# Query rotation on GpSimd, v's token shift inside the first key choice, the third gate pair as rounded products

## The reference

```python
p = x @ w_in                                   # attention, gate and RWKV columns
c_q = rms_norm(cq_raw, g_cq)
q  = partial_rope((c_q @ w_uq).reshape(B, S, 8, 128), *rope_a)   # first 32 of 128 rotated
qi = partial_rope((c_q @ w_iq).reshape(B, S, 8, 64), *rope_i)
score = sum over heads of relu(qi . ki) * wi ; _, idx = lax.top_k(score, 64)
y_a = softmax(q . k[idx]) @ v[idx] @ w_oa
p_rw = p + (prev_token(p) - p) * mu            # token shift of r, k, v, w, a, g
y_b = rwkv7_time_mix(...)                      # the recurrence, in rounds below
g_a, g_b = sigmoid(p_gate + b_gate)            # 2 x 1024 gate columns
x = layer_norm(alpha * x + (g_a * y_a + g_b * y_b) @ w_out)
x = layer_norm(alpha * x + conv_glu_ffn(x))
```

## Time and profile before

| | |
|---|---|
| median of 3 runs | 1107.33 us |
| the profiled execution, its own time | 1107.22 us |
| span of the profile, first to last instruction | 1105.4 us |
| TensorE busy | 1077.7 us, 97% |
| VectorE busy | 802.7 us, 73% |
| ScalarE busy | 569.6 us, 52% |
| GpSimd busy | 72.2 us, 7% |
| mean granted TensorE clock | 0.995 of full speed |

### The profile page before, as it was taken

How to read it: one execution, slowest core, us unless ns; L and a number is a source line. 1 busy time by engine, 2 the same in 40 slices (tenths; PEclk the granted TensorE clock), 3 DMA queues, 4 the chain that set the end, 5 groups by cost and what they waited for, 6 DMA issues and landing times. The chain is left out here.

```text
span 1105.4 us, 31915 instructions
## 1 busy us (share of the span) xinstructions
PE 1077.7 (97%) x13568; PEld 977.2 (88%) x13568; DVE 802.7 (73%) x1471; ACT 569.6 (52%) x1008; POOL 72.2 (7%) x61
## 2 busy tenths in 40 slices
PE   8999999999999999999999999999999999999996
PEld 8878888888997999998898888888888979999885
DVE  3678787868676877774557887878876778777645
ACT  3653555555544555553246445555565445555531
POOL 0000010101001000000100000202011010000001
PEclk9999999999999999999999999999999999999998
DMA  8533232322564666566474323222326637566661
GB/s 302 166 102 118 72 101 80 95 90 89 191 229 135 211 190 189 186 200 197 134 236 142 121 88 98 89 86 81 98 64 229 210 128 226 189 185 189 210 188 56
DMA packets 45526, 165.58 MB, mean 150 GB/s; under 512 B 5168, under 2 KB 5424, under 8 KB 45136
## 3 DMA queue, kind: packets, MB, share of 16 engines
q1 hardware_dynamic: 42736, 154.03, 43.4%
q0 software_dynamic: 1504, 7.47, 2.2%
q10 hardware_dynamic: 1152, 2.10, 0.6%
HBM read 160.44 MB, written 3.15 MB: 148 GB/s over the span
## 5 line engine op out<-in xcount | busy, mean ns | idle before, releaser
L771 PE MATMUL ps<-x_tok_r,mid_hi 128*128 128x256 f32 x576 | 177.1, 307 | 0.5 <-DVE ring_r L1758 0.5
L773 PE MATMUL ps<-x_tok_r,ring_r 128*128 128x256 f32 x576 | 162.2, 282 | 0.0
L772 PE MATMUL ps<-yb_hi,mid_hi 128*128 128x256 f32 x576 | 162.1, 281 | 0.0
L1758 DVE TENSOR_TENSOR ring_r<-ring,mid_hi 128x1024 fp32r<-128x1024 f32 x80 | 97.2, 1216 | 31.1 <-ACT mid_hi L1342 31.0
L771 PEld LDWEIGHTS ps<-x_tok_r,mid_hi 128*128 128x128 f32 x576 | 108.5, 188 | 9.5 <-issue 1.4
L772 PEld LDWEIGHTS ps<-yb_hi,mid_hi 128*128 128x128 f32 x576 | 108.9, 189 | 0.7 <-issue 0.7
L773 PEld LDWEIGHTS ps<-x_tok_r,ring_r 128*128 128x128 f32 x576 | 108.9, 189 | 0.0
L1342 ACT CAST mid_hi<-ring 128x1024 fp32r<-128x1024 f32 x80 | 83.8, 1048 | 34.3 <-PE ps L773 26.6
L2021 DVE TENSOR_TENSOR rs_ks_r<-ring,tha_kkn_r 128x1024 fp32r<-128x1024 f32 x44 | 53.9, 1224 | 19.9 <-ACT tha_kkn_r L1394 19.7
L2021 DVE TENSOR_TENSOR vs_dC_r<-ring,b_k_r 128x1024 fp32r<-128x1024 f32 x44 | 53.7, 1220 | 17.6 <-ACT b_k_r L1394 17.6
L2021 DVE TENSOR_TENSOR X_Y_r<-ring,arc_r 128x1024 fp32r<-128x1024 f32 x42 | 51.3, 1222 | 19.8 <-ACT arc_r L1394 19.8
(11 more groups left out here) (487 smaller groups left out, 3326.0 us busy)
## 6 DMA issues: line engine op xcount, KB each, us to landing
ring<-stream_dram SPq DMA_DIRECT2D x281, 512.0 KB, 3.7
lora_w<-lora_dram POOLq DMA_DIRECT2D x2, 1536.0 KB, 7.2
W_bt<-rpar_dram POOLq DMA_DIRECT2D x4, 512.0 KB, 5.1
kt_V<-rpar_dram POOLq DMA_DIRECT2D x4, 512.0 KB, 7.1
x_tok<-x_dram SPq DMA_DIRECT2D x2, 512.0 KB, 4.7
v_saved_dram<-vs_dC ACTq DMA_DIRECT2D x4, 256.0 KB, 4.5
x_tok<-x_dram SPq DMA_DIRECT2D x1, 1024.0 KB, 6.2
vf<-v_saved_dram ACTq DMA_DIRECT2D x4, 256.0 KB, 3.8
```

The lines of the kernel that those rows point to most:

```text
L771: pe.matmul(dst, lh, rh, start=start, stop=False)
L772: pe.matmul(dst, lh, rl, start=False, stop=False)
L773: return pe.matmul(dst, ll, rh, start=False, stop=stop)
L1758: dve.tensor_tensor(rounded["ring"][:, k, :], ring[:, k, :], f32(mid_hi[m % NM][:, :]), ALU.subtract).then_inc(*dve_mid.inc(l, m))
```

## The change

Constants: `PLAIN_GATES = 2` is new; `MIDS` takes gate slots from 4 on (6 before), so the third gate pair is multiplied in the rounded way, and `FIRST_MIDS` is 10 (8 before). The two additional splits stand on ACT behind the exponentials and ahead of the first gate's tanh; on DVE the first is in the middle of the second key choice, the second right behind it and ahead of `prep_keys`. The two rotations of the queries go from DVE to POOL, which reads and writes the same buffers; TensorE's wait ahead of the query transposes is on POOL. v's token shift, which stood ahead of the first key choice, is now done ahead of its sixth step.

```diff
-FIRST_MIDS = 2 + 3 * GB
+PLAIN_GATES = 2
+FIRST_MIDS = 2 + 3 * GB + 2 * (GATES_FIRST - PLAIN_GATES)
...
-MIDS = [s for s in SLOTS if s[1] == "gate" and s[2] >= 2 * GATES_FIRST or s[1] == "rkv" and s[2] % KB >= GB
+MIDS = [s for s in SLOTS if s[1] == "gate" and s[2] >= 2 * PLAIN_GATES or s[1] == "rkv" and s[2] % KB >= GB
...
+            def queries(l, j):
+                pool.wait_ge(*act_att(l, f"q{j}"))
+                pool.wait_ge(*(pool_att(l, "rq0") if j else dve_att(l, "rqi")))
...
+                pool.tensor_tensor(t[0], x1, cos, ALU.mult)
+                pool.tensor_tensor(t[1], x2, sin, ALU.mult)
+                pool.tensor_tensor(t[2], x2, cos, ALU.mult)
+                pool.tensor_tensor(t[3], x1, sin, ALU.mult).then_inc(*pool_att.inc(l, f"rq{j}a"))
+                pool.wait_ge(*pool_att(l, f"rq{j}a"))
+                pool.tensor_tensor(x1, t[0], t[1], ALU.subtract)
+                pool.tensor_tensor(x2, t[2], t[3], ALU.add).then_inc(*pool_att.inc(l, f"rq{j}"))
...
+                queries(l, 0)
+                queries(l, 1)
                 head_norm(GROUPS * l)
...
-                pe.wait_ge(*dve_att(l, "rq1"))
+                pe.wait_ge(*pool_att(l, "rq1"))
...
                 prep_exp(r0)
+                mids_up_to(l, FIRST_MIDS)
                 gate(l, 0)
...
-                    queries(0)
                     scores_of(4)
                     scores_of(5)
-                    queries(1)
...
-                rkv(l, 0, 2)
...
-                topk(0)
+                topk(0, lambda: rkv(l, 0, 2))
...
-                topk(1, lambda: prep_rn(r0))
+                topk(1, lambda: (prep_rn(r0), mids_up_to(l, FIRST_MIDS - 1)))
+                mids_up_to(l, FIRST_MIDS)
                 prep_keys(r0)
```

More of the change, by code:

```diff
@@ L532, in trunk @@
                                          + scores(0) + scores(1)
-                                         + (scores(2) + scores(3) + rope("rq0") + scores(4) + scores(5) + rope("rq1") if l else
-                                            rope("rq0") + scores(2) + scores(3) + rope("rq1") + scores(4) + scores(5))
+                                         + scores(2) + scores(3) + scores(4) + scores(5)
                                          + sum([[f"causal{t}"] + sum([[f"max{t}{i}", f"rep{t}{i}"] for i in range(8)], [])
@@ L538, in trunk @@
                                          for l in L2])
-        pool_att = by_layer("pool_att", ["eps", "rs"])
+        pool_att = by_layer("pool_att", ["eps", "rs"] + rope("rq0") + rope("rq1"))
         pe_prep = Steps(sem("pe_prep"), [(["ss", "zw", "za"] if r % GROUPS else ["zw", "za", "ss"]) + (["zv"] if r >= GROUPS else []) + ["rnT", "rnx"]
@@ L664, in norm_rsqrt @@
                                        ).then_inc(*pool_x.inc(l, f"{w}{t}"))
+            def queries(l, j):
+                pool.wait_ge(*act_att(l, f"q{j}"))
+                pool.wait_ge(*(pool_att(l, "rq0") if j else dve_att(l, "rqi")))
+                n = TT * 4 * 16
+                t = [yt[:, :, :].rearrange("p u s -> p (u s)")[:, 0:n], sq[:, :, :].rearrange("p u s -> p (u s)")[:, 0:n],
+                     *[X_Y[:, i, :, :].rearrange("p u s -> p (u s)")[:, 0:n] for i in range(2)]]
+                t = [a.rearrange("p (t h f) -> p t h f", t=TT, h=4) for a in t]
+                sin, cos = [sines[:, i, :, 0:16].unsqueeze(2).broadcast_to([P, TT, 4, 16]) for i in range(2)]
+                qv = q_tok[j].rearrange("p t (h f) -> p t h f", h=4)
+                x1, x2 = qv[:, :, :, 0:16], qv[:, :, :, 16:32]
+                pool.tensor_tensor(t[0], x1, cos, ALU.mult)
[5 more added lines that the diff above has]
+                pool.tensor_tensor(x2, t[2], t[3], ALU.add).then_inc(*pool_att.inc(l, f"rq{j}"))
             def head_norm(r):
@@ L1598, in _ @@
                     scores_of(3)
-                    mids_up_to(l, FIRST_MIDS)
+                    mids_up_to(l, 2 + 3 * GB)
                     queries(0)
@@ L2242, in index_queries @@
                     rotate(l, "rqi", qv[:, :, :, 0:8], qv[:, :, :, 8:16], 16, 8, H_IDX).then_inc(*dve_att.inc(l, "rqi"))
[L2244 to L2248, removed]
                 def scores_of(i):
```

## The result

The changed kernel takes 1114.57 us, the median of 7 runs (1112.53 to 1116.35), against 1106.68 us for the kernel before in the same comparison (7 runs, 1104.95 to 1110.11). The ratio is 1.0066, interval 1.0047 to 1.0085: slower by 5.2 to 9.4 us. A second comparison of the same two kernels gave 1.0056 [1.0036, 1.0077]. The forecast was slower, 1111.5 us; the measured median lies 0.4 us above the upper end of its range. The profiled execution took 1113.22 us, its span is 1111.4.

A forecast was written before the change was run, and what follows sets the result against it. TensorE's list was taken to set the time, with DVE's chain level beside it; 1.0 + 0.1 + 1.23 + 1.8 = +4.1 us on the median 1107.33 gave 1111.5 us, range 1109.3 to 1114.2.

The forecast's parts named there:

- The DVE chain: DVE's list up to the keys: 2.30 us of subtractions less 1.07 gained; +1.0 us in layer 0, +1.23 in layer 1.
- The products: Third gate pair on TensorE: rounded products save 0.69 us per slot, 2.8 in all, but the saving turns into waiting.
- POOL: Query rotations on POOL take 3.3 us per half; TensorE waits 0.1 us in layer 0 and 1.8 in layer 1.
- The sum: All waits over both layers: 1.0 + 0.1 + 1.23 + 1.8 = +4.1 us.
- rival 1: POOL's second-half rotation and DVE's sums in layer 0 exclude each other, up to 2.1 us: 1113.6 us; chance 0.15.
- Rival 2: POOL rotates as quickly as DVE, 1.42 us per half, so neither layer waits for it: +2.2 us, 1109.5; chance 0.18.
- Rival 3: DVE not held by TensorE's steps; second key choice begins 2.4 us earlier: 1106.9 or 1108.9 us; chance 0.04.

The follow-up runs named there:

- a3: Kernel before with only the third gate pair as rounded products, both subtractions on DVE, rotations and v's shift as before: ratio 1.0072.
- b2: Changed kernel with the third gate pair's two subtractions on POOL instead of DVE: ratio 1.0023 against the kernel before.
- b3: Changed kernel with the two subtractions on POOL and the second query half's rotation back on DVE: ratio 1.0002 against the kernel before.
- c1: Changed kernel; in layer 0 DVE's sums of s4 and s5 wait until POOL has rotated the second query half: one execution, 1116.05 us.
- a1: Kernel before with one edit, v's token shift moved into the first key choice: ratio 0.9992.
- c3: a1 run once more, unaltered: ratio 0.9992 against the kernel before.
- a2: Kernel before with both query rotations on POOL, nothing else changed: ratio 1.0000.
- c2: Kernel before, third gate pair plain, with two long-fulfilled waits ahead of each of its 16 products in both layers: ratio 0.9996.
- b1: Changed kernel with the second query half rotated on DVE again, the first half still on POOL: ratio 1.0065 against the kernel before.
- b4: Changed kernel with 60 long-fulfilled semaphore waits at the very start of TensorE's list: ratio 1.0074 against the kernel before.
- a4: Kernel before with 96 long-fulfilled semaphore waits in TensorE's list while it waits for the first input: ratio 1.0021.
- d1: The changed kernel unaltered, run once more: ratio 1.0056 against the kernel before.

## Why the prediction was right, and where its size was off

**The DVE chain.** The forecast was 1.0 us for layer 0 and 1.23 for layer 1. In layer 0 1.25 in all were measured, of which 0.11 are POOL, so 1.14; in layer 1 2.49 less 1.23 for POOL, so 1.26. The second key choice began near where it was put (78.83, less the later start of 0.37 is 78.46; forecast 78.30), held by the sums of squares. The first one ended 0.5 us later than forecast (75.28 - 0.37 = 74.91 against 74.4), since DVE's sums and the first row behind them were slower beside POOL; that used up the wait for the tanh in layer 0 and cost nothing more. a3 shows the same from the other side: without the rotations' gain the two subtractions cost 2.15 and 2.28 us, that is their 2.30 less the small slack of layer 0. b2 and b3, where DVE is rid of them, turn the sign in layer 0 (-1.03 and -1.19).

**The products.** 24 of them took from 86.84 to 89.7 us, 2.9 us as forecast, with a wait of 0.39 us between the slots and 1.56 ahead of the grams; the forecast was 0.5 and 1.7.

**POOL.** The sum's terms were 0.1 us for layer 0 and 1.8 for layer 1; measured 0.11 and 1.23. The term of layer 1 was too large: undisturbed, a sum of 128 elements takes no longer than a product, and steps are 0.42 us each, 2.67 us for a half, where the line from the 128x512 rows gave 3.3. POOL's first and last row of that half in layer 1 of the changed kernel:

```profile
614.08 0.46 POOL L677 TENSOR_TENSOR yt<-gates,sines 128x128 f32<-128x128 f32 x1 [1.92 <-ACT gates L1592]
...
616.29 0.46 POOL L683 TENSOR_TENSOR gates<-X_Y 128x128 f32<-128x128 f32 x1
```

That layer 0 was right was luck: there the half took 3.28 us because DVE's sums lay beside it. So rival 1 is real in kind, at 0.6 us and not 2.1, and hardly visible in the total since TensorE arrives at that moment anyway. The Trainium skill, SBUF — State Buffer, section Who interferes with whom, calls the contention on the ports that VectorE and GpSimd share an exclusive lock. c1 shows the contention. But if each of the four DVE operations of 0.5 us had locked POOL out for its whole length, POOL would have lost nearly 2 us (an estimate from these rows), and it lost 0.6.

**The sum.** +4.1 was forecast for the stages and +3.7 came. The failed step is one sentence: "From the first gram on all engines keep their order, so nothing gives that back." Nothing gave it back, but something was added: I counted no cost behind the grams. All seven timed comparisons of kernels with a rounded third pair, the changed one twice, are 2.5 to 4.9 us over their stages, 3.6 on average; the four with a plain one and no changed start (a1 and its repeat c3, a2, c2) are -0.4 to 0.2 over. The intervals are 1.3 to 2.7 us to a side, yet the two groups do not overlap.

The gaps in which TensorE waits for its own list are most of this excess. The one behind the grams of layer 0, 0.23 to 1.40 us, is in all eight profiles with rounded products ahead of them and in none of the others. All such gaps together are 3.3 us in the changed kernel and 2.1 in its repeat, 2.5 in a3, 3.5, 2.3, 2.5 and 5.0 in b1 to b4; against 1.6 in the kernel before, 0.9 in a1 and c3, 0 in a2 and 1.5 in c2 (2.6 in a4). That is 3.0 us on average against 1.0, so about 2 of the 3.6 us (an estimate, from one profile each). A second part is a wait of TensorE for DVE's `yt` (L1986, L1964 before) near 307 us in layer 0: 0.5 to 1.3 us in all eight, none in the plain kernels other than a4; the same wait in layer 1 is 0.3 us shorter on average, so 0.5 us net. About 1 us is not located. The granted clock does not make the excess: over their timed runs a3 and d1 had 0.997 and 0.996 on average, and the kernel before 0.995 beside both.

**The rivals.** Rival 2 (POOL as quick as DVE) fell: 2.67 us against 1.42. Rival 3 fell: the rows show DVE waiting 0.70 us for the exponential and 0.27 us for the sums of squares, the two things it would have to be free of.

**A better version.** b3, in which the stages gain 2.3 us, only equals the kernel before. The best measured is a1, v's shift alone: 0.9992 twice, with upper ends of 1.0004 and 1.0005, so it is better than before only by its stages, 1.1 us; the timed runs don't show it.

## What to carry to other kernels

When two engines' lists are level at a join, shortening one alone gains nothing: ask which wait on the freed engine comes next, since here 0.91 us of 2.84 got through in layer 0 (79.37 - 78.46; forecast 1.07). Split work that a faster matmul needs (rounded parts) is priced on the engine that splits, at the place where it stands in that engine's list; a third engine that idles there (b2) turned +1.25 us into -1.03. Compare stages from a common row as well as totals: the stages met the expectations to 0.3 us where the timed ratio could not, and their difference showed a cost that no stage held. And an edit that only makes an engine's list longer moves every place at which that engine waits for more of its list: where 256 rows go by in less than some 4 us, look for such a gap before blaming the edit's own work.

## What the runs showed of the hardware

- POOL's TENSOR_TENSOR in float32: 128x128 takes 0.45 us, 0.42 from start to start, product and sum alike; 128x1024 with rounded output 2.3 us; the 128x512 sum 1.62 to 1.71 us and the product 1.28.
- With DVE operations of two SBUF inputs beside it a 128x128 operation on POOL takes 0.50 to 0.64 us; DVE's 128x256 sums go from 2.11 to 2.50 us for four, and a 128x1024 subtraction beside POOL's took 1.47 instead of 1.22.
- TensorE's list reaches it in packets of 16,384 bytes, one for 256 rows of the trace; it passed none of 1498 such places less than 1.16 us after the packet had landed, and 52 gaps of 0.15 to 1.40 us end 1.19 to 1.57 us after one. The same gap was 0.83 and 0.63 us in two executions of one kernel.
- Another gap of some 0.5 us without a named releaser stands near 275 and near 825 us in every kernel, at no such place; its cause is not shown.
- 96 waits on a semaphore that has long its value are 48 rows on TensorE's queue, 0.106 us each; they put off its first matmul by 1.3 us. 60 waits (b4) were over before the first input came and put off nothing.
